# Three-operation input normalization by VectorE in a two-layer mixer trunk, with the opening's modulation one group ahead

## What is computed

```python
def rmsnorm(x, g):
    xf = x.astype(jnp.float32)
    y = xf * lax.rsqrt(jnp.mean(xf * xf, axis=-1, keepdims=True) + EPS)
    return (y * g.astype(jnp.float32)).astype(x.dtype)

def modulate_in(x, g, shift, scale):
    return rmsnorm(x, g) * (1 + scale) + shift

def trunk_layer(xl, xc, c, c_ctx, lp, li, need_ctx):
    ...
    xl = xl + 0.5 * ml[2] * swiglu(modulate_in(xl, g[0], ml[0], ml[1]), f_in[0], f_out[0])
    xc = xc + 0.5 * mc[2] * swiglu(modulate_in(xc, g[0], mc[0], mc[1]), f_in[0], f_out[0])
    ol, oc = token_mixer(modulate_in(xl, g[1], ml[3], ml[4]), modulate_in(xc, g[1], mc[3], mc[4]), lp, li, need_ctx)
    xl = xl + ml[5] * ol
    xl = xl + 0.5 * ml[8] * swiglu(modulate_in(xl, g[2], ml[6], ml[7]), f_in[1], f_out[1])
    ...
```

## Time and profile before

| | us |
|---|---|
| median of 3 runs | 2981.73 |
| lowest and highest run | 2978.26, 2985.12 |
| profiled execution | 2984.2 |
| its span, first to last instruction | 2982.3 |
| TensorE busy | 2811.9 (94%) |
| VectorE busy | 1656.6 (56%) |
| ScalarE busy | 855.1 (29%) |
| GpSimd busy | 288.3 (10%) |

### The profile page before, as it was taken

The page is one execution under the profiler, slowest core; times in us unless marked ns, Lnnn a source line. Parts: engine busy times, 40 slices in busy tenths (PEclk is TensorE's granted clock), DMA queues, the critical chain, the costliest instruction groups (busy, mean ns, idle before and its releaser), DMA issues.

```text
span 2982.3 us, 40582 instructions
## 1 busy us (share of the span) xinstructions
PE 2811.9 (94%) x15120; PEld 2536.6 (85%) x15120; DVE 1656.6 (56%) x2836; ACT 855.1 (29%) x1156; POOL 288.3 (10%) x297
## 2 busy tenths in 40 slices
PE   5999999999987889999999899999997997999998
PEld 4999999989844579999999799999986943788887
DVE  3666667659726657666766662222247736533334
ACT  4221122241355442211221422112232256432232
POOL 1000000015322100000000100000004323000000
PEclk8999999999997899999999999999998998899999
DMA  5333233321211013333333232111212311123222
GB/s 205 105 128 130 95 133 125 122 72 55 61 32 46 29 50 120 135 112 114 114 140 105 71 120 75 53 64 63 73 48 86 81 27 41 57 85 107 88 99 87
DMA packets 64418, 264.99 MB, mean 89 GB/s; under 512 B 9025, under 2 KB 11969, under 8 KB 54849
## 3 DMA queue, kind: packets, MB, share of 16 engines
q1 hardware_dynamic: 52800, 188.56, 18.7%
q0 software_dynamic: 11520, 75.11, 7.6%
HBM read 252.89 MB, written 2.10 MB: 86 GB/s over the span
## 4 chain that ended last, share of the span: by engine, by line
PE 86%; DVE 7%; ACT 3%; issue 2%; POOL 1%; DMA 0%; SPq 0%; ACTq 0%; DVEq 0%; POOLq 0%
PE ps L1626 78%; DVE conv_acc L1341 2%; PE ps L1883 1%; PE ps L1949 1%; POOL e_sb L658 1%; PE ps L1891 1%; PE ps L1931 1%; DVE w_lo L1079 1%; DVE nmax L1449 1%; PE ps L1914 1%; PE ps L1654 1%; DVE e_sb L1476 1%; DVE y_hi L1169 1%; DVE y_lo L1171 1%; PE ps L1880 0%
## 5 line engine op out<-in xcount | busy, mean ns | idle before, releaser
L1626 PE MATMUL ps<-y_hi,w_hi 128*128 128x384 f32 (+2 forms) x3184 | 909.0, 350 | 76.0 <-DVE w_lo L1079 34.5
L1626 PE MATMUL ps<-y_hi,w_lo 128*128 128x384 f32 (+2 forms) x3184 | 897.5, 346 | 0.0
L1626 PE MATMUL ps<-y_lo,w_hi 128*128 128x384 f32 (+2 forms) x3184 | 895.3, 345 | 0.0
L1626 PEld LDWEIGHTS ps<-y_hi,w_hi 128*128 128x128 f32 x3184 | 586.3, 191 | 113.7 <-issue 33.5
L706 ACT ACTIVATE w_hi<-w_raw 128x1024 fp32r<-128x1024 f32 (+1 forms) x290 | 326.6, 1128 | 1037.8 <-PE ps L1626 1037.8
L1626 PEld LDWEIGHTS ps<-y_lo,w_hi 128*128 128x128 f32 x3184 | 590.2, 191 | 21.8
L1626 PEld LDWEIGHTS ps<-y_hi,w_lo 128*128 128x128 f32 x3184 | 590.7, 191 | 20.4 <-issue 0.2
L1079 DVE TENSOR_TENSOR w_lo<-w_raw,w_hi 128x1024 fp32r<-128x1024 f32 (+1 forms) x290 | 388.2, 1339 | 301.3 <-ACT w_hi L706 298.2
L1094 DVE SCALAR_TENSOR_TENSOR mod_acc<-mod_raw,cact,mod_acc 128x256 f32<-128x256 f32 x896 | 360.2, 480 | 0.0
L1626 PE MATMUL ps<-h_hi,w_hi 128*128 128x384 f32 (+2 forms) x1254 | 353.7, 341 | 0.0
L1626 PE MATMUL ps<-h_hi,w_lo 128*128 128x384 f32 (+2 forms) x1254 | 351.7, 340 | 0.0
(11 more groups left out here) (199 smaller groups left out, 1887.0 us busy)
## 6 DMA issues: line engine op xcount, KB each, us to landing
w_raw<-in_w_up SPq DMA_DIRECT2D x176, 512.0 KB, 3.3
mod_raw<-in_w_mod POOLq DMA_DIRECT2D x64, 1024.0 KB, 5.1
w_raw<-in_w_down SPq DMA_DIRECT2D x64, 704.0 KB, 4.1
w_raw<-in_w_in SPq DMA_DIRECT2D x36, 512.0 KB, 3.2
mod_start<-in_w_mod SPq DMA_DIRECT2D x8, 1024.0 KB, 17.4
w_raw<-in_w_out SPq DMA_DIRECT2D x16, 512.0 KB, 3.2
stack<-qk_hi SPq DMA_DIRECT2D x48, 96.0 KB, 2.1
band<-in_rpb POOLq DMA_DIRECT2D x16, 224.0 KB, 6.6
```

The lines of the kernel that those rows point to most:

```text
L1626: mm = pe.matmul(slot[s][:, at:at + b - a], w[s][:, k, :], r[:, k, a:b], start=(opens and n == 0), stop=(closes and n == 2))
```

## The change

1. **Three operations.** For both halves VectorE multiplies x by scale1 and by the spread roots in one operation, ScalarE adds the shift while it writes y_hi, and VectorE adds the shift and subtracts y_hi in one operation to get y_lo. The four buffers form one ring (normed). The copy of the roots to SBUF, ScalarE's scaling into its own buffer, the cast and GpSimd's multiplications are gone.
2. **Roots.** The second half has its own place for the roots (rquads). In a last pair norm_spread(0) stands behind product kc // 3 + 4 of unit 0's second half (of 11 products in a down phase, 8 in mix_out) instead of behind its last. norm_spread(1) stands ahead of step 5 instead of 6, invert_root(1) behind chunk 4 instead of 5.
3. **Opening.** first_mods is cut in two, the 16 matmuls (first_mods) and the turn (first_turn). Groups 0 and 1 are done ahead of the first product, with the sums and spreads of both halves between them; the 16 matmuls of groups 2 and 3 stand behind chunks 1 and 3, their turns behind chunks 2 and 4. ScalarE copies the rows of group j + 1 between the two halves of chunk 2j. VectorE waits for both spreads at the start.
4. **ScalarE at an up phase.** A Silu of one column (load_silu) behind the last y_hi takes the table load; behind the first pair of an up phase the w_hi split of unit 0 stands ahead of the real Silu.

```diff
     sq = [place(f"sq{s}", [P, TOK]) for s in range(2)]
+    normed = [sq[0], act_buf, sq[1], hid_buf]
...
+    rquads = [rstd[:, 0:LAT // 4], rstd[:, LAT // 4:LAT // 2]]
...
-                for m in range(DC):
-                    if m >= 2:
-
-                        pool.wait_ge(sems["affine"], 2 * DC * (norms[0] - 1) + DC + m - 1 if norms[0] > 1 else 2 * m - 2)
-                    pool.tensor_tensor(sq[m % 2][:, a:b], x[:, m, a:b], rstd[:, a:b], ALU.mult).then_inc(sems["normed1"], 1)
...
-            def copy_spread(tokens):
-
-                a, b, _ = halves(tokens)[1]
-                t.wait("spread1")
-                act.activation(rstd[:, a:b], spread[1][:, 0:b - a], ACT.Copy).then_inc(sems["rstd_copied"], 1)
...
+                    act.activation(y_hi[:, m, a:b], normed[m % 4][:, a:b], ACT.Identity,
+                                   bias=mod_vec[:, k, shift + m:shift + m + 1]).then_inc(sems["y_hi"], 1)
...
+                if norm != 1:
+                    load_silu()
...
+                act.activation(warm[:, :], eps_t[:, 0:1], ACT.Silu)
...
+                    opening = p.after_norm and isinstance(i, int) and i == 0
+                    if opening:
+                        split_hi(p, i, 0, ahead)
...
+                        dve.scalar_tensor_tensor(normed[m % 4][:, a0:b0], x[:, m, a0:b0], scale1[:, k0, m:m + 1], spread[0][:, 0:b0 - a0],
+                                                 ALU.mult, ALU.mult).then_inc(sems["normed0"], 1)
...
+                        dve.scalar_tensor_tensor(y_lo[:, m - 1, a0:b0], normed[(m - 1) % 4][:, a0:b0], mod_vec[:, k0, shift + m - 1:shift + m],
+                                                 y_hi[:, m - 1, a0:b0].bitcast(F32), ALU.add, ALU.subtract).then_inc(sems["y_lo"], 1)
...
-                    if m == 5:
+                    if m == 4:
                         invert_root(p.tokens, 1)
...
-                        if s == 1 and k == 0:
+                        if s == 0 and k == p.kc // 3 + 5:
                             norm_spread(p.tokens, 0)
...
-                            if k % 2 == 0 and k < DC - 2:
-                                first_mods(1 + k // 2)
+                            if k in (1, 3):
+                                first_mods(2 + k // 2)
+                            if k in (2, 4):
+                                first_turn(1 + k // 2)
...
-                                if half == 0 and step == 6 and pair0:
+                                if half == 0 and step == 5 and pair0:
                                     norm_spread(p.tokens, 1)
```

More of the change, by code:

```diff
@@ L718, in root @@
                 t.wait("norm_sum")
[L719 to L725 removed]
+                act.activation(rquads[half][:, 0:q], roots[half][:, 0:q], ACT.Sqrt, bias=eps_t[:, 0:1], scale=1.0 / D).then_inc(sems["norm_sqrt"], 1)
             def make_y(layer, norm, tokens, after=None):
@@ L730, in make_y, with load_silu @@
                 shift = mod_chunk(layer, 3 * norm)
[L731 to L737, removed]
-                        act.activation(buf[:, a:b], sq[m % 2][:, a:b], ACT.Identity,
-                                       bias=mod_vec[:, k, shift + m:shift + m + 1],
-                                       scale=scale1[:, k, m:m + 1]).then_inc(sems["affine"], 1)
-                        t.wait("affine")
[L742 to L745, removed]
+                a, b, k = halves(tokens)[0]
+                for m in range(DC):
+                    t.wait("normed0")
+                    act.activation(y_hi[:, m, a:b], normed[m % 4][:, a:b], ACT.Identity,
+                                   bias=mod_vec[:, k, shift + m:shift + m + 1]).then_inc(sems["y_hi"], 1)
+                    if after:
+                        after(m)
+                a, b, k = halves(tokens)[1]
+                for m in range(DC):
+                    t.wait("normed1")
+                    act.activation(y_hi[:, m, a:b], normed[m % 4][:, a:b], ACT.Identity,
+                                   bias=mod_vec[:, k, shift + m:shift + m + 1]).then_inc(sems["y_hi"], 1)
+                if norm != 1:
+                    load_silu()
                 y_made[0] += 2 * DC
+            def load_silu():
+                act.activation(warm[:, :], eps_t[:, 0:1], ACT.Silu)
             y_made = [0]
@@ L1145, in make_scale, with make_y @@
                 ins.then_inc(sems["scale_ready"], 1)
-            def make_y(tokens, after=None):
-                (a0, b0, _), (a1, b1, _) = halves(tokens)
+            def make_y(layer, norm, tokens, after=None):
+                (a0, b0, k0), (a1, b1, k1) = halves(tokens)
+                shift = mod_chunk(layer, 3 * norm)
+                t.wait("scale_ready")
                 t.wait("spread0")
@@ L1163, in make_y @@
                     if after:
                         after(m)
[L1165 to L1172 removed]
+                t.wait("spread1")
@@ new lines, in make_y @@
+                for m in range(DC + 1):
+                    if m < DC:
+                        if m >= 4:
+                            dve.wait_ge(sems["y_lo"], y_made[0] + DC + m - 3)
+                        dve.scalar_tensor_tensor(normed[m % 4][:, a1:b1], x[:, m, a1:b1], scale1[:, k1, m:m + 1], spread[1][:, 0:b1 - a1],
+                                                 ALU.mult, ALU.mult).then_inc(sems["normed1"], 1)
+                    if m:
+                        t.wait("y_hi")
+                        dve.scalar_tensor_tensor(y_lo[:, m - 1, a1:b1], normed[(m - 1) % 4][:, a1:b1], mod_vec[:, k1, shift + m - 1:shift + m],
+                                                 y_hi[:, m - 1, a1:b1].bitcast(F32), ALU.add, ALU.subtract).then_inc(sems["y_lo"], 1)
@@ L1653, in norm_spread @@
                     row, rows = (pick[:, g - 1, :], P) if g else (ones[0:1, :], 1)
-                    mm = pe.matmul(spread[half][:, q * g:q * g + q], row, rquad[0:rows, 0:q], start=True, stop=True)
+                    mm = pe.matmul(spread[half][:, q * g:q * g + q], row, rquads[half][0:rows, 0:q], start=True, stop=True)
                 mm.then_inc(sems[f"spread{half}"], 1)
```

86 lines of the change are left out of this document (33 added, 53 removed).

## The result

The changed kernel takes 2965.3 us, the median of four runs (2964.76 to 2970.07), beside 2982.6 for the kernel before on the same chip; the ratio is 0.9942 with an interval of 0.9930 to 0.9953. That is 17.3 us less where 31 were forecast, and 1.3 us above the top of the range for 8 in 10 (2941 to 2964). The profiled execution has a span of 2968.4 us, 13.9 less than that of the kernel before.

A forecast was written before the change was run, and what follows sets the result against it. TensorE's own work is 86% of the chain of waits, so only its stalls and half clock at six normalized inputs could give; the places sum to -31.4, taken as -31, from median 2981.7 to 2950.7 us; 8-in-10 range 2941 to 2964.

The forecast's parts named there:

- (a): Rival: gains hanging on the clock fail; opening -4, place 6 -2, the rest -17, so -23 us, 2959; chance 0.19.
- place 1: The opening: modulation products one group ahead; next pair starts at 72.6 to 76.2 us, -6.7 to -10.3, taken as -8.5.
- Places 2 to 4: Layer 0's mix_in (-2.5 us), the up phase behind it (-4.5), and the up phase that opens layer 1 (-4.3).
- the second half: Second half's normalization in a last pair: VectorE needs 0.8 us a chunk with GpSimd silent; -1.2 us a place.
- the end of the first half: Root copy ahead of chunk 7 goes, TensorE's wait with it: -1.1 us, with 0.2 from the front -1.3 a place.
- Place 5: Layer 1's mix_in: second half's y_lo, memset and w_lo come earlier, shortening TensorE's wait of 7.13 us; -5.6 us.
- Place 6: Last up phase (512 tokens): -7.6 us if full clock comes back, -2.1 if it stays at 1.2 GHz; taken as -6.
- The head of an up phase: Behind its first pair: early table load and w_hi ahead of Silu, 2.4 us instead of 4.4; -2.0 us a place.
- The front: Start of each place: the earlier spread of the first roots is worth about its own stall; counted 0.
- Rival (c): VectorE streams the new y_lo at half pace, +0.53 us a chunk at 512 wide; -2 us in all, 2980; chance 0.03.
- (b): Rival: the front gains, roots 1 us earlier shorten waits and keep the clock up; -39 us, 2942; chance 0.12.
- (d): Rival: frequent short gaps hold TensorE at 1.2 GHz through each whole first pair; +22 us, 3004; chance 0.03.

The follow-up runs named there:

- a_shift0: Changed kernel with the table load's one-element tensor put in a spare element of eps_t, so later buffers keep their old addresses: 2943.9 us; timed again, 2946.5 us.
- a_h32: a_shift0 with only the product operands h_hi and h_lo placed 32 bytes higher: one run, 2952.2 us.
- the four variants: a_shift0 without early table load, 2952.0 us; with w_hi behind Silu, 2955.5; with both undone, 2959.0; kernel before with only both moves, 2977.6.
- a0_no_load: a_shift0 without the early load of the Silu table, so the first Silu of an up phase loads it: 2952.0 us.
- a0_spread_late: a_shift0 with the spread of the first half's roots back behind unit 0 of the last pair: 2947.4 us.
- a_shift64: Changed kernel with the new tensor made 64 bytes large, so everything behind it stands 64 bytes higher than before the change: 2946.5 us.

## Why the prediction was wrong, and where it was right

**The step that failed** is in the part-by-part costing: it goes through the new operations, their order and the table load, and says nothing of the tensor the load writes. It was taken for free without being named, and its 32 bytes of layout cost 13 to 17 us, twice what the forecast and its nearest rival (a) lie apart (8). In the table the steady stretches and the last stage make +14.8 us in the changed kernel and +1.8 and +1.0 in a_shift0: 13 to 14 us, most of the miss. (The forecast had scaled 0.233 us for 512 columns from 384; the kernel before takes 0.227 there and the changed one 0.233, so that number hid the loss.) The rest of it (+3.9 us, less 1.3 behind place 1), and most of what a_shift0 has over the forecast (-6.5), lies in the mixers, where the forecast counted 0 and the half-clock stretches fell otherwise.

**The places**, which are all that the prediction argued, sum to -31.3 and -36.3 in the two profiles of the changed kernel and to -33.5 and -31.7 in those of a_shift0, against -31.4. Without the tensor the median is 2943.9 and 2946.5 us against 2950.7 forecast, inside the range of 2941 to 2964. That the changed kernel's own places sum to -31.3 is in part luck, as the terms show:

- Place 1, 74.07 us, at the middle of 72.6 to 76.2; the other profile had 70.1. Two errors cancel in it. The clock was full from the first product (0.62 us for two, where 1.01 is half clock), which the steps had put at half clock for chunk 0; and that product came at 36.23, not 34.8, because the modulation products and spreads ahead of it ran at half pace (3.20 us for 16 products, where the other profile has 1.92 and starts at 32.73).
- Places 2 to 4: no wait ahead of chunk 7, second halves unbroken. Place 3's 4.5 is 3.1 three times and 4.7 once, place 4's 4.3 is 3.6 to 7.4. In place 3 the second half gave 1.5 us (1.2 forecast) and the head 2.0 in all four. The 1.3 at the end of the first half came once, with 3.4 us of half clock in the place; with 6.8 us, in the other three, that stretch took 0.3 us more than before, though the wait was gone. Place 4 goes by half clock too: 29.2 us with none of it, 29.9 with 3.4 us (a_h32), 30.6 and 32.3 with 6.8 and 33.0 with 10.2. The forecast sized one number for a place that the clock spreads over 4 us.
- Place 5: -5.6, -6.1, -5.6, -5.5 for -5.6, with a wait of 1.84 us for about 2.6.
- Place 6: -5.6 to -6.7 for -6, with 7 to 10 us at half clock for 13.7 before: it did come back.
- The head of an up phase, a gap of 0.6 instead of 2.4 (1.8, where the sum took 2.0): 0.45 for 2.40 in place 3, and the two chains that the text added up (w_lo at 2.4, Silu at 2.0) are the ones that the four variants found.
- The front: chunk 1's first product in place 2 starts at 620.27, 0.2 us later than in the kernel before (0.3 in a_shift0) if both are counted from the last product ahead of the spread; nothing gained, as counted.

**Prices.** The new multiplication and the new y_lo take 0.75 us at 512 wide and 0.48 at 256 (0.749 and 0.485 taken). Rival (c), the Trainium skill's rule of half throughput for two SBUF sources that aren't bf16 (Vector Engine (DVE) Microarchitecture Reference, Points that are easy to get wrong), is not what the trace shows. ScalarE's operation with the bias alone takes 0.72 us where I took 0.65 between 0.63 and 0.81. The Trainium skill (ScalarE: Activation LUTs, What ACT_TABLE_LOAD costs) says that each operand given as a column adds some 93 ns; 0.63, 0.72 and 0.81 agree with it. The drain of 1.38 us that it adds to a table switch shows nowhere: in a0_no_load the load starts 0.02 us behind the end of w_hi, and Silu 1.29 us behind the load's start.

**Rivals.** (a) gave the nearest time, 2959, for a reason that didn't happen: the parts of the opening and of place 6 that hang on the clock came. (b) fell with a0_spread_late. (c) and (d) didn't happen.

## What to carry to other kernels

A new tensor, however small, moves everything placed behind it: write down the places of TensorE's moving operands before and after an edit, and keep them where they ran fast (here multiples of 128 bytes from the first tensor, and 64 off is nearly as good), for instance by putting a stray element into a spare place. When a change gains what it should at each place and the total falls short, compare the same instruction's start in both traces stretch by stretch; the loss here lay in loops that the diff doesn't touch. And where two chains end at nearly the same time, the two moves that shorten them must be priced together.

## What the runs showed of the hardware

- A moving operand of 512 fp32 columns moved up by 32 bytes makes a product take 233 ns instead of 227, each product by its own operand (a_h32); moved up by 64 bytes it is 229 (a_shift64). At 384 columns the loss is small, 1.5 us in the 476 us between places 1 and 2, and none at all in the 370 us of unbroken products ahead of place 5 (41.6 us for 240 of them in both).
- The granted clock in stretches of broken work differs from one execution of a program to the next: 27 and 38 us of half clock in the second mixer of one and the same kernel, 3.3 us of time; 0 and 10 us in its place 4, 3.8 us of time. A forecast made from one profile can be off by several us for this reason alone.
